# First expert step placed among the last scatter groups, last coefficient tile stored from the ScalarE queue, own buffers for two steps

## What is computed

```python
idx = jnp.take_along_axis(cand_i, best_pos, axis=-1)      # 1024 tokens x 8 heads x 16 experts of 16384
gates = jax.nn.softmax(best_s, axis=-1)
def one_block(args):
    h_blk, idx_blk, g_blk = args
    u = jnp.take(expert_u, idx_blk, axis=0)
    act = jax.nn.gelu(jnp.einsum('thkd,td->thk', u, h_blk))
    vv = jnp.take(expert_v, idx_blk, axis=0)
    return jnp.einsum('thk,thkd->td', g_blk * act, vv)
```

## Time and profile before

| | us |
|---|---|
| median of 3 runs (lowest, highest) | 3231.39 (3228.85, 3231.85) |
| the profiled execution | 3233.7 |
| its span, first to last instruction | 3232.0 |
| PE, DVE, ACT, POOL busy in the span | 3032.2, 2463.1, 1094.7, 1202.0 |
| scatter stage ends (last copy into sc_w) | 1377.6 |
| first share of the loop begins | 1460.1 |

### The profile page before, as it was taken

The page is one execution under the profiler, slowest core; times in us unless marked ns, Lnnn a source line. Parts: engine busy times, 40 slices in busy tenths (PEclk is TensorE's granted clock), DMA queues, the critical chain, the costliest instruction groups (busy, mean ns, idle before and its releaser), DMA issues.

```text
span 3232.0 us, 52539 instructions
## 1 busy us (share of the span) xinstructions
PE 3032.2 (94%) x18277; PEld 2699.4 (84%) x18277; DVE 2463.1 (76%) x4967; ACT 1094.7 (34%) x2027; POOL 1202.0 (37%) x966
## 2 busy tenths in 40 slices
PE   6999999899799869869999999999999999999996
PEld 4998888789678759858898889888888988988895
DVE  5455333374489989968888888888888888888887
ACT  4222666503345645522222222222222222222222
POOL 0001000010067700045555555555555555555551
PEclk9999999999899979989999999999999999999998
DMA  6435433133301028899888888988888899889885
GB/s 239 151 126 180 111 107 106 72 130 112 105 27 44 13 76 253 265 333 335 318 317 322 327 318 320 336 307 325 320 325 315 319 331 329 313 318 340 317 303 214
DMA packets 350575, 760.99 MB, mean 235 GB/s; under 512 B 20620, under 2 KB 175848, under 8 KB 350448
## 3 DMA queue, kind: packets, MB, share of 16 engines
q0 software_dynamic: 115712, 419.48, 36.1%
q1 hardware_dynamic: 233680, 335.65, 30.6%
q10 hardware_dynamic: 1056, 4.19, 0.3%
HBM read 686.86 MB, written 72.39 MB: 235 GB/s over the span
## 4 chain that ended last, share of the span: by engine, by line
PE 53%; DVE 5%; issue 2%; DMA 2%; DVEq 2%; ACT 0%; POOL 0%; ACTq 0%; POOLq 0%; SPq 0%
PE psum L2062 23%; PE psum L2069 22%; PE psum L1285 3%; PE psum L2054 2%; PE psum L1794 2%; DMA ex_un<-in_expert_u 1%; DVE ex_u_row L2267 1%; DVE acc L2280 1%; DVEq L2277 1%; DVEq L2270 1%; DMA ex_v_row<-in_expert_v,ex_row 0%; PE psum L1267 0%; DVE acc L2320 0%; DVE ex_g L2300 0%; DVE h_lo L2257 0%
## 5 line engine op out<-in xcount | busy, mean ns | idle before, releaser
L2011 POOL DMA_INDIRECT ex_u_row<-in_expert_u,ex_row x384 | 450.0, 1172 | 898.6 <-DVE ex_dot L2267 602.5
L2011 POOL DMA_INDIRECT ex_v_row<-in_expert_v,ex_row x384 | 510.3, 1329 | 153.0 <-issue 110.6
L2280 DVE SCALAR_TENSOR_TENSOR acc<-ex_v_row,ex_coef,acc 128x1024 f32<-128x1024 f32 x384 | 492.6, 1283 | 37.1 <-DMA ex_v_row<-in_expert_v,ex_row 9.5
L2267 DVE CUSTOM_DVE_ANT_0 ex_u_row<-ex_u_row,h_rows 128x1024 f32<-128x1024 f32 x384 | 466.8, 1216 | 4.1 <-DMA ex_u_row<-in_expert_u,ex_row 3.8
L2069 PE MATMUL psum<-ex_v_hi,ex_c_lo 128*128 128x512 f32 x1260 | 360.4, 408 | 18.8 <-DVE ex_v_lo L2262 8.3
L2069 PE MATMUL psum<-ex_v_lo,ex_c_hi 128*128 128x512 f32 x1260 | 339.2, 391 | 0.0
L2069 PE MATMUL psum<-ex_v_hi,ex_c_hi 128*128 128x512 f32 x1260 | 338.5, 390 | 0.0
L2062 PE MATMUL psum<-h_hi,h_lo 128*128 128x320 f32 x1792 | 300.2, 310 | 17.2 <-DVE h_lo L2257 17.2
L2062 PE MATMUL psum<-h_lo,h_hi 128*128 128x320 f32 x1792 | 300.2, 310 | 0.0
L2062 PE MATMUL psum<-h_hi 128*128 128x320 f32 x1792 | 300.0, 310 | 0.0
L2062 PEld LDWEIGHTS psum<-h_hi,h_lo 128*128 128x128 f32 x1792 | 275.0, 188 | 22.7 <-DVE h_lo L2257 13.9
(11 more groups left out here) (347 smaller groups left out, 5354.5 us busy)
## 6 DMA issues: line engine op xcount, KB each, us to landing
ex_vn<-in_expert_v SPq DMA_DIRECT2D x64, 1024.0 KB
ex_un<-in_expert_u SPq DMA_DIRECT2D x48, 1024.0 KB
w_dram<-sc_w SPq DMA_DIRECT2D x10, 4096.0 KB, 14.9
ex_w<-w_dram SPq DMA_DIRECT2D x64, 640.0 KB
gm_wm<-in_w_mod SPq DMA_DIRECT2D x16, 1024.0 KB, 5.3
pj_raw<-in_w_in SPq DMA_DIRECT2D x11, 1024.0 KB, 8.6
qk_dram<-pj_staged_r POOLq DMA_DIRECT2D x32, 256.0 KB, 2.9
gt_raw<-in_w_in SPq DMA_DIRECT2D x16, 512.0 KB, 3.9
```

Source lines behind the costliest of these rows:

```text
L2011: nc.gpsimd.indirect_dma_start(to[:], None, all_rows, bass.IndirectOffsetOnAxis(row[s][:, col:col + 1], 0)).then_inc(done, 16)
L2267: nc.vector.tensor_tensor_reduce(out=u_row[k % 3][:], in0=u_row[k % 3][:], in1=h_rows[:, k % 3, :], scale=1.0, scalar=0.0, op0=ALU.mult, o ...
L2280: nc.vector.scalar_tensor_tensor(out=to, in0=v_row[k % 3][:], scalar=coef[:, k:k + 1], in1=to, op0=ALU.mult, op1=ALU.add).then_inc(row_use ...
```

## The change

It has four parts. (1) The turn and the hides of step 0 are moved from behind the scatter stage into it: the turn stands behind group 36, hide units 0, 1 and 2 behind groups 37, 38 and 39, the high parts on ACT behind group 36's copies, the low parts on DVE behind group 37's one-hot tiles. The load of step 0's `ex_un` moves from behind group 35's store to just behind the store of tile 7 (group 31); the load of step 1's stands behind group 39. (2) The store of tile 9 is issued by ACT instead of SP. (3) The gelu results of steps 0 and 1 get eight tiles of their own (`ex_first`), so they need neither `ex_pre` nor one another's space; four lie in space that is free by then, four where `sc_w` 0 was. (4) On DVE, ACT and SP the work between the scatter stage and the loop is put in another order: step 1's low parts ahead of the first row dots, five pairs of gathered rows before step 2's low parts, `weigh` and `lower` of steps 0 and 1 behind them, and step 2's `ex_un` loaded before the coefficients. The loop itself is the same. Core of the diff:

```diff
@@ class Scatter: vector, tensor, scalar, sync each get then(g) at the end of a group @@
+            if g == self.GROUPS - 1:
+                act.wait_ge(self.evicted, 4 * self.GROUPS)
+                self.store(act, self.TILES - 1)
+            then(g)
...
-            if g == self.GROUPS - self.NG:
-                next_u(sp)
-            if g % self.NG == self.NG - 1:
+            if g % self.NG == self.NG - 1 and tile < self.TILES - 1:
                 sp.wait_ge(self.evicted, 4 * (g + 1))
...
+    first_out = [[core.at(f"ex_first{j}{n}", kb + 1.25 * n, [P, HD]) for n in range(4)] for j, kb in enumerate((180, 0))]
+    FIRST_TURN = scatter.GROUPS - scatter.NG
@@ sync @@
+                if g == FIRST_TURN - scatter.NG - 1:
+                    load_u(sp, 0, 0, True)
+                if g == scatter.GROUPS - 1:
+                    load_u(sp, 0, 1)
             sp.wait_ge(scatter.placed, scatter.GROUPS)
             load_v(sp, 0, 0)
+            load_u(sp, 0, 2)
             scatter.stored_all(sp)
             load_w(sp, 0, 0)
             load_w(sp, 1, 1)
-            load_u(sp, 0, 2)
             load_w(sp, 2, 0)
@@ tensor @@
+            def among(g):
+                if g == FIRST_TURN:
+                    pe.wait_ge(ahead.lo_out, 2 * ahead.BLOCKS + 2)
+                    pe.wait_ge(ahead.gelued, 2 * ahead.BLOCKS + 2)
+                    for q in range(4):
+                        turn(0, 0, q, q)
+                elif g > FIRST_TURN:
+                    if g == FIRST_TURN + 1:
+                        u_split(0, 0)
+                    hide(g - FIRST_TURN - 1, g - FIRST_TURN - 1)
+            scatter.tensor(pe, among)
+            hide(3, 3)
@@ scalar @@
+            def among(g):
+                if g == FIRST_TURN:
+                    split_u(0, 0, range(4))
+                elif g > FIRST_TURN:
+                    if g == scatter.GROUPS - 1:
+                        indices(0, 2)
+                        indices(0, 0)
+                    first_gelu(0, g - FIRST_TURN - 1)
+            scatter.scalar(act, among)
+            first_gelu(0, 3)
+            split_u(0, 1, range(4))
+            gelu_dots(0, 0)
+            act.wait_ge(scatter.stored[0], scatter.TILES // 2 * 16)
+            for n in range(4):
+                if n == 3:
+                    gelu_dots(0, 1)
+                first_gelu(1, n)
+            indices(1, 1)
+            split_u(0, 2, SECOND_BANKS)
...
+            for j in range(2):
+                for n in range(4):
+                    upper(0, j, n, True)
+            split_v(0)
+            gelu_dots(1, 0)
+            gelu_dots(1, 1)
+            indices(2, 0)
+            gelu(0, 2, HIDE_BANKS[0])
@@ vector @@
+            def among(g):
+                if g == FIRST_TURN + 1:
+                    for q in range(4):
+                        split_u(0, 0, q, q)
```

More of the change, by code:

```diff
@@ L1764, in pairs, with vector @@
             [P, self.G // 2, NKEYS, 2])
-    def vector(self, dve):
+    def vector(self, dve, then):
         nc = self.nc
@@ L1807, in tensor, with scalar @@
                     ahead.leave(pe, n, m)
-    def scalar(self, act):
+            then(g)
+    def scalar(self, act, then):
         ahead = self.ahead
@@ L1828, in scalar, with store, sync @@
                 (ahead.upper if g % 3 == 1 else ahead.lower)(act, *self.job(k + 1))
-    def sync(self, sp, next_u):
+            if g == self.GROUPS - 1:
+                act.wait_ge(self.evicted, 4 * self.GROUPS)
+                self.store(act, self.TILES - 1)
+            then(g)
+    def store(self, eng, tile):
+        eng.dma_start(self.t.w_dram[:, :, tile:tile + 1, :].rearrange("c j b n -> j c (b n)"),
+                      self.w[tile % 2][:].rearrange("p (c e) t -> p c (e t)", e=2)).then_inc(self.stored[tile % 2], 16)
+    def sync(self, sp, then):
         ahead = self.ahead
@@ L1908, in x @@
     def x(j, n, first=False):
-        return act_out[n % 2] if n < 2 or (not first and j % 2 == 0) else pre[n % 2]
+        if first:
+            return first_out[j][n]
+        return act_out[n % 2] if n < 2 or j % 2 == 0 else pre[n % 2]
     def v_flat(v):
@@ L2114, in step @@
                         share(s, n, core.bank[4 + 2 * n + dh], True, v)
[L2116 to L2119, removed]
+            def among(g):
[10 more added lines that the diff above has]
+            hide(3, 3)
             for j in range(2):
-                u_split(0, j)
-                for n in range(4):
-                    hide(n, n)
+                if j == 1:
+                    u_split(0, 1)
+                    for n in range(4):
+                        hide(n, n)
                 for q in range(4):
@@ L2162, in split_last_v, with first_gelu @@
                 nc.scalar.activation(h.hi[:, 0:2, :], v_flat(vn), ACT.Copy).then_inc(v_hi, 1)
[L2164 to L2170, removed]
+            def first_gelu(j, n):
+                act.wait_ge(hidden, 4 * j + n + 1 + PRIME)
+                nc.scalar.activation(x(j, n, True)[:], core.bank[n][:, 0:HD], ACT.Gelu_apprx_tanh).then_inc(gelued, 1)
             def upper(i, j, n, first=False):
@@ L2339, in hides, with among @@
                         pair(c + 2, 3 + n)
-            for q in range(4):
-                split_u(0, 0, q, q)
+            def among(g):
+                if g == FIRST_TURN + 1:
+                    for q in range(4):
+                        split_u(0, 0, q, q)
+            scatter.vector(dve, among)
+            dve.wait_ge(scatter.evicted, 4 * scatter.GROUPS)
+            nc.vector.memset(core.psum[:, 4:8, :].rearrange("p b n -> p (b n)"), 0.0).then_inc(cleared, 1)
             dve.wait_ge(scatter.stored[0], scatter.TILES // 2 * 16)
             nc.vector.memset(acc[:, KEPT:TT, :].rearrange("p t d -> p (t d)"), 0.0)
+            for q in range(4):
+                split_u(0, 1, q, q)
             dve.drain()
@@ L2348, in _ @@
                 dve.drain().then_inc(row_used, 1)
+            for k in range(5):
+                pair(0, k)
             for q in range(4):
-                split_u(0, 1, q, q)
+                split_u(0, 2, q, SECOND_BANKS[q])
+            for j in range(2):
+                for n in range(4):
+                    weigh(0, j, n, True)
+                    lower(0, j, n, True)
+            split_v(0)
+            pair(0, 5)
             for k in range(3):
-                pair(0, k)
+                pair(1, k)
             for n in range(4):
-                weigh(0, 0, n, True)
-                lower(0, 0, n, True)
-            hides(0, -2)
+                weigh(0, 2, n)
+                if n < 3:
+                    pair(1, 3 + n)
+                lower(0, 2, n)
             def step(i, j, banks, turns, hiding=True):
```

28 lines of the change are left out of this document (5 added, 23 removed).

## The result

The changed kernel takes 3238.12 us (median of 17 runs, 3233.08 to 3239.48), the one before, run beside it, 3231.39 (17 runs, 3227.97 to 3236.34). The medians lie 6.7 us apart. The ratio, which is worked out from all the runs and not from the two medians, is 1.0017, 95% interval 1.0011 to 1.0024: about 5.5 us slower. 3224.4 was forecast. The profiled execution has a span of 3236.5 us, before 3232.0.

A forecast was written before the change was run, and what follows sets the result against it. PE bounds the loop, so only its start could move: DVE 3.1 + 3.0 = 6.1 us early, hides of step 3 8 early, 7 taken. That gave 3226.7 from 3233.7 profiled, 3224.4 against the median 3231.39; range 3215 to 3233.

The forecast's parts named there:

- DVE's sum up to the coefficients: DVE between scatter stage and loop: three pairs end at 1411.8, step 2's low parts start at 1419, end at 1421.5.
- the coefficient tile: Before DVE's first weigh: `ex_w` arrives between 1412 and 1426, taken as 1418 to 1421, no wait; range's end costs 5 us.
- Rival D: At the first weigh: queues take turns, store lands at 1431, `ex_w` at 1436.5, 7.5 us slower, 3239; chance 0.08.
- rival C: At the first weigh: store lands at 1415 to 1424, DVE stands until 1429, gain 4 to 0, about 3230; chance 0.17.
- The 7 us of gain: At the loop's start: DVE 6.1 us early, PE's hides of step 3 8 us early; 7 us taken.
- The 3.1 us on DVE: At the first low part of step 3: DVE arrives at 1458.8, 3.1 us before its old time.
- the 3.0 us behind it: On DVE, first low part of step 3 to next v split: old waits for PE and ACT, 1.78 and 1.26, vanish.

The follow-up runs named there:

- e2: Changed kernel with the load of `ex_vn` moved behind the two `ex_w` loads, tile 9's store left on ACT's queue: 3231.58 us, ratio 1.0005.
- c6: Changed kernel with `ex_vn` loaded late, three pairs before step 2's low parts, six among the weighings, store on ACT: 3224.31 us, ratio 0.9977.
- e4: Kernel before with only tile 9's store moved from SP's queue to ACT's: 3235.20 us, ratio 1.0017.
- c5: Changed kernel with store on SP, `ex_vn` late, three pairs before step 2's low parts, six among the weighings: 3228.39 us, ratio 0.9989.
- e1: Changed kernel with tile 9's store put back on SP's queue, ahead of `ex_vn`: 3232.92 us, ratio 1.0008.

## Why the prediction was wrong

**Right.** The scatter stage: last copy into `sc_w` at 1382.07 (forecast 1381.1). PE's turn of step 1 at 1388.58 (near 1388). DVE's sum up to the coefficients: the three pairs ended at 1412.8 (1411.8), step 2's low parts began at 1419.75 (1419). The loop's busy times did not change. Without its 6.26 us wait the first low part of step 3 would stand 120.87 - 6.26 = 114.6 us after tile 7's store; the sum gave 1458.8 - 1344.26 = 114.5.

**The step that failed** is the coefficient tile: "26.2 us by the row gives 1407; plus both loads, 1413; if it is last of all that is queued, 1421 ... I take 1418 to 1421, no wait". The store landed at 1424.0, past the bound that I had called the end, and DVE waited. The working added bytes, as if all transfers shared one pipe. The engines take turns by packet: from 1403 to 1407 in the changed kernel

```profile
q0 software_dynamic: 389, 1.40, 86.3%
q10 hardware_dynamic: 391, 0.20, 16.7%
```

the store had as many packets as the gathers and a seventh of their bytes, since its runs are 512 B and theirs 4 KB: 0.05 MB/us. It moved fast only where the gathers paused or ran thin (1484 packets for their 216 from 1411 to 1415). Rival D had this mechanism and 3239, 1 us from the median, at a chance of 0.08. I set it aside with "the loads are over after 6 us of DMA, so the lower rate cannot last". The loads do end, but the gathers go on through the whole stretch, and I priced the rate beside them from a window in which the first three were running out and the next not yet issued (257 packets for 968). One us earlier in the same trace, from 1386 to 1390, the store had a fifth of the gathers' bytes:

```profile
q0 software_dynamic: 357, 1.27, 83.6%
q1 hardware_dynamic: 441, 0.23, 18.6%
```

D's landing at 1431 was 7 us too late, so that its 3239 was partly luck. The landing (1424.0) and the first weigh (1428.48) lie where rival C had put them (1415 to 1424, until 1429), but C gave that wait a gain of 4 to 0, and by D too a first weigh at 1429 only brings back the old time. That the kernel lost has a further reason, the next point.

**A second error, of the size.** The profile of before stood for an execution that was late in just this stretch, as far as two profiles can tell (S 132.23, and 128.95 when taken again). The 7 us of gain were reckoned against it and then taken off the median. The 3.1 us on DVE were no gain at all against the second profile (first low part of step 3 after 114.40 us there, 114.6 less the wait here). Of the 3.0 us behind it 0.7 arrived (from the first low part to the v split 13.82 us instead of 14.55), as two new waits for rows (1.42, 1.19) took the place of those for PE and ACT. So against the first profile S went by -3.1 + 6.26 - 0.7 = +2.5 us, and against the second by +5.7. e2, with no wait for `ex_w`, shows the worth of the early step in this order of DVE's list: S 128.79 against 128.95, none that can be measured.

So the loss is the 6.26 us wait, from three queues where there were two. The gain meant to pay for it was not there, because DVE's own list (pairs in sequence with their gathers, then eight 0.54 us hand-overs to ACT) fills the time that the early turn opened: up to the second v split its waits for gathered rows add up to 13.9 us, where they were 1.3 before. c6 shows that the changed order can pay once that list is shortened. Whether the early turn has a part in that gain is not shown: no run spreads the pairs in the kernel before.

## What to carry to other kernels

In this kernel a store of small runs could not be priced by bytes while it shared the DMA engines with transfers of large runs on other queues. In such a case count packets in turn, and look whether the large ones ever pause. Moving it to a queue of its own freed what stood behind it and slowed the store itself, so first ask who waits for its landing and move the loads that nobody needs yet behind it. And where an engine holds both long independent work and short hand-overs to another engine, put the one into the gaps of the other before moving work between stages; and profile the kernel before twice when the gain looked for is 0.2%.

## What the runs showed of the hardware

- The queues' equal turns, in three kernels: 389 packets to 391, 385 to 385 (next window of the changed kernel), 227 to 221 to 225 (e4), 291 to 293 (the kernel before, 1402 to 1406).
- A 4 MB store in 512 B runs needs 14.9 us alone, 18.4 to 26.2 ahead of the loads in SP's queue, and 24.7 to 41.9 on a queue of its own, by what the others carry.
- A 1 MB load behind such a store in the same queue took 6.67 us (c5) to 15.46 us (e1) to issue, and 0.37 us in the changed kernel with the store in another.
- DVE stood 0.54 us (0.62 the first time) at each hand-over of a 128x320 tile to ACT and back (`weigh`, `upper`, `lower`), and none where a pair stood between (c6).
